# Taking four weight tiles of a state space stage from the input before its norm, on one Trainium2 core

## The reference, cut to what matters

```python
def rmsnorm(x, w):
    y = x * rsqrt(mean(x * x, axis=-1) + 1e-6)
    return y * w
h = rmsnorm(x, norm_mix_w)
proj = h @ w_in                      # 1024 -> 8224 columns
(ssm_z, ssm_xbc, ssm_dt, gdn_qkv, gdn_z, gdn_a, gdn_b, gate_ssm, gate_gdn) = split(proj)
xbc = silu(causal_dwconv(ssm_xbc, conv_w) + conv_b)      # 4 taps over tokens
dt = softplus(ssm_dt + dt_bias);  g = -exp(a_log) * softplus(gdn_a + dt_bias);  beta = sigmoid(gdn_b)
y_ssm = chunked state space scan(xs * dt, dt * a, B, C)
```

## Time and profile before

| | |
|---|---|
| time of before, median of 3 runs | 3094.06 us (3093.57 to 3095.58) |
| span of the profiled execution (first to last instruction) | 3089.4 us |
| PE busy | 2977.7 us, 96% of the span |
| DVE, ACT, POOL busy | 1605.5, 1078.7, 1412.1 us |
| mean granted TensorE clock | 0.988 of full |
| first matmul of the first dense tile | 26.89 us |
| data moved | 248 MB, 80 GB/s |

### The profile page before, as it was taken

How to read it: one execution, slowest core, us unless ns; L and a number is a source line. 1 busy time by engine, 2 the same in 40 slices (tenths; PEclk the granted TensorE clock), 3 DMA queues, 4 the chain that set the end, 5 groups by cost and what they waited for, 6 DMA issues and landing times.

```text
span 3089.4 us, 42486 instructions
## 1 busy us (share of the span) xinstructions
PE 2977.7 (96%) x16912; PEld 2385.2 (77%) x16912; DVE 1605.5 (52%) x3295; ACT 1078.7 (35%) x1781; POOL 1412.1 (46%) x1817
## 2 busy tenths in 40 slices
PE   6998999999999999999999999999899999999999
PEld 5777777787888887767877778888776768788887
DVE  5766567566566416559744453330466773433310
ACT  4443333333322223323324433222354553332221
POOL 3553344344556544314334364555543334655554
PEclk9999999999999999999999999999999999999999
DMA  3211112112344432102112222333321112232232
GB/s 123 83 55 60 57 55 69 55 56 82 117 149 144 129 96 66 36 21 69 36 48 75 69 82 96 96 94 101 101 69 61 58 59 81 84 96 96 97 103 88
DMA packets 72358, 248.02 MB, mean 80 GB/s; under 512 B 8160, under 2 KB 8544, under 8 KB 72032
## 3 DMA queue, kind: packets, MB, share of 16 engines
q1 hardware_dynamic: 72160, 245.30, 24.8%
HBM read 243.18 MB, written 2.10 MB: 79 GB/s over the span
## 4 chain that ended last, share of the span: by engine, by line
PE 84%; DVE 12%; ACT 2%; issue 1%; POOL 1%; DMA 0%; SPq 0%; DVEq 0%; ACTq 0%; POOLq 0%
PE bank L1054 23%; PE bank L1056 22%; PE bank L1055 22%; PE bank L1088 3%; PE bank L1102 3%; PE bank L1533 1%; PE bank L1065 1%; PE bank L1551 1%; DVE sm L1617 1%; DVE sm L1619 1%; PE bank L1542 1%; PE bank L1372 1%; DVE sm L1621 1%; POOL t L2943 1%; DVE t L1764 1%
## 5 line engine op out<-in xcount | busy, mean ns | idle before, releaser
L2910 POOL TENSOR_TENSOR R<-W,R 128x256 fp32r<-128x256 f32 x1715 | 1287.9, 784 | 1540.5 <-ACT R L2518 1540.5
L1054 PE MATMUL bank<-u,R 128*128 128x512 f32 (+1 forms) x3440 | 1393.9, 405 | 27.2 <-DVE u L1720 8.3
L1056 PE MATMUL bank<-u,R 128*128 128x512 f32 (+1 forms) x3440 | 1348.8, 392 | 0.0
L1055 PE MATMUL bank<-u,R 128*128 128x512 f32 (+1 forms) x3440 | 1347.8, 392 | 0.0
L1054 PEld LDWEIGHTS bank<-u,R 128*128 128x128 f32 (+1 forms) x3440 | 649.2, 189 | 182.5 <-issue 15.9
L1056 PEld LDWEIGHTS bank<-u,R 128*128 128x128 f32 (+1 forms) x3440 | 648.6, 189 | 142.4 <-issue 0.4
L1055 PEld LDWEIGHTS bank<-u,R 128*128 128x128 f32 (+1 forms) x3440 | 650.3, 189 | 127.5 <-issue 4.8
L2518 ACT ACTIVATE R<-W 128x1024 fp32r<-128x1024 f32 (+2 forms) x454 | 452.3, 1002 | 143.3 <-PE bank L1056 136.8
L2548 ACT ACTIVATE u<-t 128x512 fp32r<-128x512 f32 x126 | 78.3, 630 | 322.9 <-DVE t L1742 249.1
L1753 DVE SCALAR_TENSOR_TENSOR X<-bank,X 128x512 f32<-128x512 f32 x32 | 22.1, 692 | 260.2 <-PE bank L1056 260.2
L1720 DVE TENSOR_TENSOR u<-t,u 128x512 fp32r<-128x512 f32 x126 | 97.3, 782 | 100.5 <-ACT u L2548 99.8
(11 more groups left out here) (389 smaller groups left out, 2748.4 us busy)
## 6 DMA issues: line engine op xcount, KB each, us to landing
W<-in_in SPq DMA_DIRECT2D x48, 512.0 KB, 3.3
W<-in_ff_in SPq DMA_DIRECT2D x44, 512.0 KB, 3.3
W<-in_g_qkv SPq DMA_DIRECT2D x24, 512.0 KB, 3.3
W<-in_ada SPq DMA_DIRECT2D x24, 512.0 KB, 3.3
W<-in_f1g SPq DMA_DIRECT2D x22, 512.0 KB, 3.3
W<-in_f1u SPq DMA_DIRECT2D x22, 512.0 KB, 3.2
W<-in_f2g SPq DMA_DIRECT2D x22, 512.0 KB, 3.2
W<-in_f2u SPq DMA_DIRECT2D x22, 512.0 KB, 3.3
```

Of the source, the lines that this page charges most:

```text
L1054: e.matmul(b[0:cols, :], wh, hi, start=(k == 0), stop=False)
L1055: e.matmul(b[0:cols, :], wh, lo, start=False, stop=False)
L1056: i = e.matmul(b[0:cols, :], wl, hi, start=False, stop=(k == KT - 1))
L2910: i = e.tensor_tensor(R[q % NH][:, 1024 + a:1024 + b], W[p % NW][:, a:b], R[q % NH][:, a:b].bitcast(F32), SUB)
```

## The change

The norm's steps are no longer ahead of the planner's list but a chain in it. A new step `xu` k forms high and low parts of x times gain, without the root (ACT Copy with a scale, and one DVE scalar_tensor_tensor, shown below), into the tiles `UX`. The dense tiles in `RAW` (small and xbc 8, 9, 10) take these as operands. For xbc 8, 9 and 10 a new step `cr` (DVE, in place in the bank) multiplies the result by the root, before `conv`; for `small` the root is applied after the transposes, in `sums` 1. The root is copied from bank 7 to a tile by ACT (`rb`). All other tiles use the operands of `h` as before; `h` now reads the root's tile. `room` lets the plan open tile 11 (the first that reads the operands of `h`) when `h` 8 has ended. The planner's clocks of DVE and ACT begin at 8 us, that of POOL at 4. `sq` and `acc` run one pair behind `xu`. SP issues the panel of `small` ahead of the first load of x and that of xbc 8 ahead of the second.

```diff
+UX = (tuple(range(21, 29)), tuple(range(33, 41)))
+RAW = (("small", 0), ("s_xbc", 8), ("s_xbc", 9), ("s_xbc", 10))
 SEG:
+    nsum="p.9", rms="v3.4", rmsp="p.45", rb="s.63", h="v1.05 s.63 g.65", cr="v.75",
 AFTER = {
+    "nsum": lambda n, k: [("nsum", 0, 6)] if k == 7 else [], "rms": lambda n: [("nsum", 0, 7)], "rmsp": lambda n: [("rms", 0)],
+    "h": lambda n, k: [("h", 0, k - 1) if k else ("rb", 0)], "rb": lambda n: [("rmsp", 0)], "cr": lambda j: [("rb", 0)],
+    "sums": lambda n: [("sums", n - 1) if n else opens("small", 0)] + [("rmsp", 0)] * (n == 1),
-    "conv": lambda which, j: [("conv2",) + CONV[which][4](j)] if CONV[which][4](j) else [],
+    "conv": lambda which, j: ([("conv2",) + CONV[which][4](j)] if CONV[which][4](j) else []) + [("cr", j)] * (CONV[which][3](j) in RAW),
 def room(name, j):
+    if (name, j) == ("s_xbc", 11):
+        return [("h", 0, 8)]
-def weave(chains, *fills):
+def weave(chains, *fills, begun_at=(0.0, 0.0, 0.0)):
-    now, out = dict(p=0.0, v=0.0, s=0.0, g=0.0), []
+    now, out = dict(p=0.0, v=begun_at[0], s=begun_at[1], g=begun_at[2]), []
 def convs(which, js):
-        out += tiles(*CONV[which][3](j), ("conv", which, j))
+        out += tiles(*CONV[which][3](j), *([("cr", j)] if CONV[which][3](j) in RAW else []), ("conv", which, j))
 def order():
-    O = [("begin",), ("ada0",), ("halves",)]
-    for k in range(8):
-        O += [("sq", 0, k)] + ([("acc", 0, k)] if 1 <= k <= 6 else [])
-    O += [("nsum", 0, 6), ("splits", 3)]
-    O += norm(0)
+    O = [("begin",), ("ada0",), ("halves",), ("splits", 1)]
+    done = 0
+    for k in range(0, 8, 2):
+        O += [("xu", k), ("xu", k + 1)] + [("splits", 2)] * (k == 0)
+        for i in range(done, k if k < 6 else 8):
+            O += [("sq", 0, i)] + ([("acc", 0, i)] if 1 <= i <= 6 else [])
+        done = k
+    O += [("splits", 3)]
+    first = [("nsum", 0, 6), ("nsum", 0, 7), ("rms", 0), ("rmsp", 0), ("rb", 0)] + [("h", 0, k) for k in range(9)]
-    O += weave([chain, normed(0) + normed(1)], convs("xbc", XORD) + convs("qkv", range(6)))
+    O += weave([first, chain, normed(0) + normed(1)], convs("xbc", XORD) + convs("qkv", range(6)), begun_at=(8.0, 8.0, 4.0))
 tensor, operand():
+                if (name, j) in RAW:
+                    w.wait_ge(*NM.dve.at("xlo", k))
+                    return r(UX[0][k]), r(UX[1][k])
 vector:
+            def xu(k):
+                w.wait_ge(*NM.act.at("xhi", k))
+                e.scalar_tensor_tensor(out=r(UX[1][k]), in0=X[:, k, :], scalar=gain(0, k), in1=r(UX[0][k]).bitcast(F32), op0=MUL,
+                                       op1=SUB).then_inc(*NM.dve.up("xlo", k))
+            def cr(j):
+                b = bank[BANK["s_xbc", j]]
+                w.wait_ge(*PN.pe.at("dense", "s_xbc", j))
+                w.wait_ge(*NM.act.at("rb", 0))
+                e.tensor_tensor(b, b, t(RB), MUL).then_inc(*CV.dve.up("root", j))
 vector, sums(1):
+                    w.wait_ge(*NM.dve.at("y", 0))
+                    after(e.tensor_tensor(raw, bank[4][:, 0:256].rearrange("p (t c) -> p t c", t=4),
+                                          small["nw"][:, 8:12].unsqueeze(2).broadcast_to([128, 4, 64]), MUL), "scaled")
 scalar:
+            def xu(k):
+                w.wait_ge(*x_ready(0, k))
+                e.activation(r(UX[0][k]), X[:, k, :], ACT.Copy, scale=gain(0, k)).then_inc(*NM.act.up("xhi", k))
 scalar, conv:
+                if (name, gj) in RAW:
+                    w.wait_ge(*CV.dve.at("root", gj))
 sync, begin():
                 for i in range(4):
+                    fetch(min(i + 1, 2))
                     e.dma_start(X[:, 2 * i:2 * i + 2, :], D["x"][:, 2 * i:2 * i + 2, :]).then_inc(s_x[i], 16)
                 fetch(NW)
```

More of the change, by code:

```diff
@@ L1031, in tensor, with operand @@
         def tensor(e, w):
-            def operand(name, k):
+            def operand(name, j, k):
+                if (name, j) in RAW:
+                    w.wait_ge(*NM.dve.at("xlo", k))
+                    return r(UX[0][k]), r(UX[1][k])
                 if name in NORM_OF:
@@ L1050, in dense @@
                     at = (j % GROUP.get(name, 1) * KT + k % 8) * cols
-                    hi, lo = operand(name, k)
+                    hi, lo = operand(name, j, k)
                     w.wait_ge(*PN.pool.at("lo", key))
@@ L1689, in h @@
                 if k < 8:
-                    w.wait_ge(*NM.pe.at("r", n))
+                    w.wait_ge(*(NM.pe.at("r", n) if n else NM.act.at("rb", 0)))
                     if n == 3:
@@ L1695, in h @@
                         w.wait_ge(*(NM.dve if k % 2 or n == 3 else NM.pool).at("lo", n, k - 3))
-                    e.scalar_tensor_tensor(out=t(SQ[k % 3]), in0=X[:, k, :], scalar=gain(n, k), in1=bank[NB[n]], op0=MUL,
+                    e.scalar_tensor_tensor(out=t(SQ[k % 3]), in0=X[:, k, :], scalar=gain(n, k), in1=bank[NB[n]] if n else t(RB), op0=MUL,
                                            op1=MUL).then_inc(*NM.dve.up("h", n, k))
@@ L1784, in sums @@
                     dtb = PC[:, PAT["dtb"][0]:PAT["dtb"][1]].unsqueeze(1).broadcast_to([128, 4, 24])
+                    raw = kcols(SUMS[3])
                     e.memset(t(K_TM)[:, 0:256], 0.0).then_inc(*SU.dve.up())
                     w.wait_ge(*SU.pe.at("tr"))
-                    after(e.tensor_tensor(z, bank[4][:, 0:256].rearrange("p (t c) -> p t c", t=4)[:, :, 0:24], dtb, ADD), "z")
+                    w.wait_ge(*NM.dve.at("y", 0))
+                    after(e.tensor_tensor(raw, bank[4][:, 0:256].rearrange("p (t c) -> p t c", t=4),
+                                          small["nw"][:, 8:12].unsqueeze(2).broadcast_to([128, 4, 64]), MUL), "scaled")
+                    after(e.tensor_tensor(z, raw[:, :, 0:24], dtb, ADD), "z")
                     after(e.scalar_tensor_tensor(out=u, in0=z, scalar=-1.0, in1=z, op0=MUL, op1=MIN), "u")
@@ L2497, in fc4 @@
                 e.scalar_tensor_tensor(out=o, in0=o, scalar=P("subln"), in1=bank[q.X], op0=MUL, op1=MUL).then_inc(*DF.dve.up("y", h))
-            do = dict(acc=acc, rms2=rms2, rms=rms, h=h, xg=xg, xscale=xscale, pair=pair, ffg=ffg, ffs=ffs, ffu=ffu, res=res,
+            do = dict(acc=acc, xu=xu, cr=cr, rms2=rms2, rms=rms, h=h, xg=xg, xscale=xscale, pair=pair, ffg=ffg, ffs=ffs, ffu=ffu, res=res,
                       conv=conv, conv2=conv2, sums=sums, xd=xd, st0=st0, st=st, ch=ch, cb=cb, cm=cm, sz=sz, sy=sy, sn2=sn2,
@@ L2584, in sums @@
                     e.activation(t(SUMS[2])[:, 96:128].rearrange("p (t c) -> p t c", t=4),
-                                 bank[4][:, 0:256].rearrange("p (t c) -> p t c", t=4)[:, :, 32:40], ACT.Tanh,
+                                 kcols(SUMS[3])[:, :, 32:40], ACT.Tanh,
                                  scale=0.5).then_inc(*SU.act.up("beta"))
@@ L2891, in ft2r @@
                 e.activation(t(q.q), t(q.q), ACT.Sqrt, scale=(1.0 - LAM_INIT) ** 2 * 2.0 ** -64).then_inc(*DF.act.up("r", h))
-            do = dict(split=split, sq=sq, h=h, rb=rb, xg=xg, pair=pair, ffg=ffg, conv=conv, conv2=conv2, sums=sums, bt=bt,
+            do = dict(split=split, sq=sq, xu=xu, h=h, rb=rb, xg=xg, pair=pair, ffg=ffg, conv=conv, conv2=conv2, sums=sums, bt=bt,
                       che=che, sz=sz, sn1=sn1, i0=i0, il=il, it=it, iu=iu, hqs=hqs, hn2=hn2, hg=hg, hs2=hs2, ho=ho, hz=hz,
```

## The result

The changed kernel takes 3103.58 us, the median of 6 runs (3100.9 to 3104.91); the kernel before takes 3093.93 us beside it, the median of 6 (3092.99 to 3095.58). The ratio is 1.0031, with a 95% interval of 1.0021 to 1.0041: 9.65 us slower. Forecast were 3102 us, +8.0, and slower with 0.53.

A forecast was written before the change was run, and what follows sets the result against it. PE was taken as full from 65.6 to 190 us, then chain-bound, so the change is worth its shift of the stage's end: 9.1 - 0.6 - 1.0 + 0.5 = +8.0, giving 3102 us; likeliest case 3098 to 3107, 8-in-10 range 3087 to 3110.

The forecast's parts named there:

- tile 11 ends late: End of tile 11 on ACT, the mark of comparison: 74.8 us against 65.7 before, +9.1, as `h` is ranked low.
- Start of PE: Start of the stage: partition sums at 20.6 us instead of 13.7, first dense matmul at 22 to 23.
- The delay through the loads: Loads of x: weights issued ahead of later pairs put them back by up to 2.1 us, taken as 1.8.
- rms: The root on DVE: takes 5.4 us from 26.9, done at 32.3.
- rmsp: The root's spread on PE: behind the third piece of tile 8, at 35.0 us, ending near 36.2.
- Softplus: Ahead of `sums` 3: Exp at 46.4 us, plus 6.2 of small steps, `sums` 3 at 52.6, PE idle 4.6.
- Order of `h`: On DVE: `h` gets its turn only when nothing else is ready; `h` 1 behind `ch` 0, at 64.3 us.
- The tail: Behind the tile 11 mark: -0.6 for `ch` 0 on PE, -1.0 for the chain, +0.5 for the clock.
- Span and median: Whole kernel: the median of the runs lies 4.7 us above the profile's span, and the same is added to the forecast.
- A: Rival, faster: `h` is not pushed back, `h` 8 done before PE finishes tile 10; 3085 to 3091 us, chance 0.17.
- B: Rival, same: tile 11 late, but 16 us of PE idle from 190 to 252 absorb it; 3093 to 3099, chance 0.23.
- C: Rival, slower still: low clock through tile 11 and one more tile, or worse plan order; 3106 to 3116 us, chance 0.12.

The follow-up runs named there:

- before_weights_first: The kernel before with only the fetch of weight panels ahead of parts of x added; 3096.57 us, ratio 1.0007.
- root_early_own: The changed kernel with the planner's DVE clock beginning at 3.0 instead of 8.0 and scratch tiles of its own for `h`; 3101.67 us, ratio 1.0021.
- h_both: The changed kernel with `h` ranked first, `h` k waiting only for `h` k-3 in the plan, and own scratch tiles; 3102.11 us, ratio 1.0027.
- x_loads_first: The changed kernel without the fetch of weight panels ahead of parts of x; 3109.85 us, ratio 1.0052.
- norm_first_quiet: The changed kernel with squares and sums first, splits of panels 1 and 2 after the root, `sums` ranked up, `h` k waiting for `h` k-3; 3094.96 us.
- before_pool_idle_in_root: The kernel before with a weight split's place in the order edited, no engine's queue changed; 3093.18 us, ratio 0.9998.

## Why the prediction was right, and where its steps were not

Right in sign, in size (8.0 forecast, 9.65 measured) and in the place: tile 11 ends late (+9.1 forecast, +11.6 measured), waits for low parts of `h`, and the full stretch behind it is only shifted. Part of this is luck: several steps missed, and their errors cancel in part. One sign that the prediction named for being right, `h` 1 on DVE behind the DVE part of `ch` 0, did not come.

- **Start of PE**: partition sums at 20.6 forecast, 21.26 measured; first dense matmul 22 to 23 forecast, 22.95 measured. The delay through the loads, sized at 1.8, is 1.4 by before_weights_first.
- **`rms`**: 5.4 forecast, 2.9 measured, because POOL is idle then. Nothing came of it, as the root then waits 7.3 us for PE.
- **`rmsp`**: its place in the queue was read rightly (behind the third piece of tile 8), the time of PE up to it was not: 35.0 forecast, 37.55 measured. Six matmuls were put at 0.43 us; measured, 17 of them come at that pace, up to 31.42. The further 11 at 0.20 more make 2.2, and the start was 0.7 later. What the prediction did not see is what this place costs: the start time that sets it is worth 6.5 us with one order of `h` and 1.9 with another.
- **Softplus**: this is the step that failed. The Exp was forecast for 46.4 and ran at 54.11. The walk through the plan put `sums` 1 ahead of `conv` 8 on DVE, and so the Exp on ACT right behind `conv` 9. On the chip DVE has `conv` 8 first, at 41.95, and `sums` 1 from 44.27, and the Exp stands behind `conv` 10, at 53.43, which waits for `cr` 10 and the end of tile 10. So ACT's queue ties the Exp to the end of a dense tile. `sums` 3 came at 59.23, not 52.6. In root_early_own, where `sums` 1 goes first and the Exp stands ahead of `conv` 9, it came at 49.64.
- **Order of `h`**: `h` 1 was forecast for 64.3, behind `ch` 0. It ran at 48.40, and `h` 2 and 3 also went ahead of `ch` 0; `h` 4 to 7 behind it. So the walk through the plan was wrong here too. With `sums` 3 at 59.23, +4.9, the later softplus and the fewer late `h` together give nearly the end that was forecast, 77.32 against 74.8.
- **A slip in the sum**: from the low part for k = 1 at 68.5 to that for k = 7 are three pairs at 2.05, which make 6.15 and not 5.3. Put right, the forecast end of tile 11 is 75.65 rather than 74.8, +9.95 rather than +9.1, and the whole +8.85. That is nearer to the 9.65 measured, though by steps that missed themselves.
- **The tail**: forecast -1.1 from `ch` ahead of the mark and the clock together; measured 2.4 given back between tile 11 and the next stage.
- **Span and median**: the 4.7 us added to the span were for the most part no property of the kernel (1.8 are in the changed kernel's profiled run). In the difference of two medians that cancels.

Of the rivals, A (faster) needed `h` 7 on DVE ahead of 50 us; it ran at 73. That point was badly chosen: in h_both all `h` are done by 54, and 1.5 us of the median came of it. B (same): of 11.6 us, 2.4 were taken up. C (slower still, the low clock through tile 11): the first six matmuls of tile 11 come every 0.43 us, those from 69.51 on every 0.23 within each group, but for the first of a group (0.34), although gaps of 1.11, 0.19, 0.96 and 0.34 us stand between the groups. The rule of the Trainium skill, page "TensorE: Matmul & The Clock Gate", section "HAM oscillation — how this bites in real kernels", by which a PE that pauses for data between short groups is throttled again each time, would, carried over to this tile, have had all 24 at 0.43. The trace does not agree for gaps of 1.11 us and less; the page's own example has longer ones, and those no tile here shows.

**What stays open.** With the norm first, 7.9 us come back, and the rest is within the scatter. How the 7.9 divide between the late partition sums, the wait in PE's queue and the new places of `sums` 1 and the Exp no run separates; the start time that moves the last three was worth 1.9 with one order of `h` and 6.5 with the other. Why x_loads_first is 6.3 us slower by its median and only 2.0 at the next stage is not settled; it had five runs, and the one with a profile was the fastest. From the next stage to its end that profile has 2843.4 us, 3.1 less than that of the changed kernel, so scatter behind the mark can cover 3.1 of the 4.3 us between the two figures.

## What to carry to other kernels

To let TensorE start on un-normalised data can pay only if the norm itself is not put back by it, and here it did not pay even then: count what the new operands cost the engines that make the norm, and look where the norm's own TensorE step stands in the queue, since a ready result behind an in-order queue holds up every engine behind it. When one edit of an order removes a wait and the time stays, look for the same microseconds at the next wait before you drop it: here two edits gave 2 us each at the mark behind the stage, and 10 together (1.5, 1.9 and 8.0 by the medians). A planner's costs and start times are part of the kernel: one start time was worth 6.5 us with one order of the rest and 1.9 with another, and it moved more steps than the one that it was meant to move.

## What the runs showed of the hardware

A VectorE instruction on four columns takes 0.17 us alone and 0.64 to 0.72 us while GpSimd runs its 0.70 us tensor_tensor instructions; on 128x512 a scalar_tensor_tensor takes 0.68 alone and 0.94 so, the two `h` of norm_first_quiet 1.15 each rather than 0.70. The small one thus waits for about one whole GpSimd instruction and takes nearly four times as long, the large one up to 1.6 times. The root's first instruction, which reads a PSUM bank, is not hit: 0.16 us at 17.27 in the kernel before, while GpSimd works from 14.01 to 20.88. GpSimd is slowed as well: the twelve splits of norm_first_quiet beside `xu` and `h` take 12.01 us, 1.00 each. The Trainium skill has the rule on the page "SBUF — State Buffer", section "Who interferes with whom": VectorE and GpSimd share a pair of ports, which the first to issue holds for its whole instruction while the other blocks, where VectorE has two inputs in SBUF or a one-input instruction such as tensor_scalar runs in a mode that uses both ports. The traces agree: the two-input instructions are hit (0.64 to 0.68), the tensor_scalar with one tensor operand too (0.66), and the one whose only input is in PSUM is not (0.16). A string of small VectorE steps on the path that sets the end is the worst place to run GpSimd beside, and to move that work pays only if it lands beside nothing that counts: 2.5 us won in the root were lost again at the next low part.

The same idle time does not always cost the clock. Ahead of `sums` 3 PE waits 3.48 us in the kernel before and 3.49 in before_pool_idle_in_root, which has the same queues. Windows of 54 to 66 us, first of the kernel before, then of the other:

```profile
54.00:66.00 12.00, 11.66 (x45) 9.65 (x46) 7.77 (x15) 4.54 (x6) 0.49 (x1) 0.73 0.13 44
```

```profile
54.00:66.00 12.00, 11.61 (x56) 9.49 (x57) 9.58 (x18) 6.33 (x11) 2.83 (x4) 1.00 0.14 44
```

PE is busy equally long, but the granted clock is 0.73 in the one (1.2 GHz up to 60.4 us, then 2.4) and 1.00 in the other (2.4 GHz throughout), which gets 56 matmuls done for 45. That is the 2.6 us at the end of tile 11. In before_weights_first, after 3.49 us of idle, the clock falls a few matmuls into `sums` 3 and is back at 59.5. So the 2.5 us of low clock that rival A meant to save are not there in every execution, and a single profile can be wrong by as much.
